# A split weight buffer of the experts, moved by 32 bytes

## The reference

```
probs = softmax(h @ router)
top_p, top_i = top_k(probs)                      # gates, made to sum to 1
for e in range(8):
    out += gates[:, e] * (silu(h @ w_gate[e]) * (h @ w_up[e])) @ w_down[e]
```

## Time and profile before

| | |
|---|---|
| timed runs | 1557.62, 1558.37, 1560.37 us (median 1558.37) |
| profiled execution, span | 1558.8 us (no time of it beside the span is recorded) |
| TensorE busy | 1525.1 us, 98% of the span |
| VectorE, ScalarE busy | 1188.6 us, 1017.6 us |
| expert stage | about 1130 to 1554 us |
| granted TensorE clock, mean | 0.995 of 2.4 GHz |

### The profile page before, as it was taken

How to read it: one execution, slowest core, us unless ns; L and a number is a source line. 1 busy time by engine, 2 the same in 40 slices (tenths; PEclk the granted TensorE clock), 3 DMA queues, 4 the chain that set the end, 5 groups by cost and what they waited for, 6 DMA issues and landing times.

```text
span 1558.8 us, 26842 instructions
## 1 busy us (share of the span) xinstructions
PE 1525.1 (98%) x9894; PEld 1308.5 (84%) x9894; DVE 1188.6 (76%) x1477; ACT 1017.6 (65%) x1431; POOL 60.4 (4%) x74
## 2 busy tenths in 40 slices
PE   7999999999999999999999999999999999999998
PEld 6988888878878888899888888998878888888886
DVE  5677877775578877787775556887688888888887
ACT  5667665566567656687465455875577777777775
POOL 0000000000000000020000000100000001101000
PEclk9999999999999999999999999999999999999999
DMA  7535455445424555464255555462699999999995
GB/s 269 195 119 189 167 211 188 177 147 189 169 102 165 213 188 184 142 190 144 80 192 187 204 181 184 162 167 83 227 373 368 394 387 381 369 396 385 364 362 210
DMA packets 54794, 351.08 MB, mean 225 GB/s; under 512 B 6208, under 2 KB 9968, under 8 KB 14896
## 3 DMA queue, kind: packets, MB, share of 16 engines
q1 hardware_dynamic: 46512, 330.94, 56.8%
q0 software_dynamic: 8192, 18.90, 4.7%
HBM read 341.90 MB, written 7.91 MB: 224 GB/s over the span
## 4 chain that ended last, share of the span: by engine, by line
PE 91%; DVE 4%; DMA 2%; ACT 2%; issue 1%; POOL 0%; SPq 0%; DVEq 0%; ACTq 0%
PE PS L917 20%; PE PS L1852 16%; PE PS L1985 14%; PE PS L2021 11%; PE PS L1870 8%; PE PS L1986 8%; PE PS L1478 1%; DVE EWL L3761 1%; PE PS L1083 1%; PE PS L1956 1%; DMA rows_m<-HN 1%; PE PS L1833 1%; DMA W<-in_weights 1%; PE PS L962 1%; PE PS L1547 1%
## 5 line engine op out<-in xcount | busy, mean ns | idle before, releaser
L3761 DVE TENSOR_TENSOR EWL<-W,EWH 128x2048 fp32r<-128x2048 f32 x144 | 329.6, 2291 | 45.4 <-ACT EWH L2789 45.2
L1985 PE MATMUL PS<-HTB,WH 128*128 128x512 f32 x944 | 329.3, 393 | 0.0
L2789 ACT ACTIVATE EWH<-W 128x2048 fp32r<-128x2048 f32 x144 | 276.5, 1920 | 61.3 <-PE PS L1870 34.2
L1986 PE MATMUL PS<-HTB,WL 128*128 128x256 f32 x1008 | 282.4, 280 | 0.0
L3087 DVE TENSOR_TENSOR WL<-W,WH 128x2048 fp32r<-128x2048 f32 x99 | 226.5, 2287 | 35.9 <-ACT WH L2216 32.8
L2216 ACT ACTIVATE WH<-W 128x2048 fp32r<-128x2048 f32 x99 | 189.2, 1918 | 95.4 <-PE PS L1986 84.6
L917 PE MATMUL PS<-MWH,HTB 128*128 128x256 f32 (+1 forms) x940 | 240.9, 341 | 2.1 <-issue 1.5
L3095 DVE TENSOR_TENSOR MWL<-W,MWH 128x1024 fp32r<-128x1024 f32 x136 | 164.5, 1220 | 85.2 <-ACT MWH L2240 83.2
L1985 PEld LDWEIGHTS PS<-HTB,WH 128*128 128x128 f32 x944 | 177.2, 188 | 40.1
L2240 ACT ACTIVATE MWH<-W 128x1024 fp32r<-128x1024 f32 x136 | 142.5, 1054 | 98.2 <-PE PS L917 89.8
L1986 PEld LDWEIGHTS PS<-HTB,WL 128*128 128x128 f32 x1008 | 189.5, 188 | 1.0
(11 more groups left out here) (413 smaller groups left out, 2441.1 us busy)
## 6 DMA issues: line engine op xcount, KB each, us to landing
W<-in_weights SPq DMA_DIRECT2D x311, 1024.0 KB, 4.9
CS<-in_consts POOLq DMA_DIRECT2D x4, 403.5 KB, 4.8
ARENA<-rows_m POOLq DMA_DIRECT2D x8, 192.0 KB, 6.2
ARENA<-rows_m POOLq DMA_DIRECT2D x2, 768.0 KB, 12.2
moe_acc<-X POOLq DMA_DIRECT2D x3, 512.0 KB, 12.1
moe_rows<-HN POOLq DMA_DIRECT2D x3, 512.0 KB, 12.1
X<-in_x SPq DMA_DIRECT2D x2, 512.0 KB, 4.4
W<-in_weights SPq DMA_DIRECT2D x2, 512.0 KB, 7.1
```

What stands on the lines that cost most here:

```text
L1985: mm(PS[b][:, :], WH[:, sl, o:o + P], HTB[:, :, kk, :], start=(kk == 0), stop=False, skip_group_check=True)
L1986: ins = mm(PS[b][:, 0:256], WL[:, sl, o:o + P], HTH[:, kk, :], start=False, stop=(kk == KC - 1), skip_group_check=True)
L2789: A(EWH[tile % SPLIT][:, :], tile_ap(w0 + tile), ACT.Copy).then_inc(sem("moe_hi"), 1)
L3761: TT(EWL[tile % SPLIT][:, :], tile_ap(w0 + tile), EWH[tile % SPLIT][:, :].bitcast(F32), SUB).then_inc(sem("moe_lo"), 1)
```

## The change

The experts' buffer 1 starts 8 floats (32 bytes) further on, both halves. To make room, every split buffer of every stage is given 16 floats more than it holds (`SHIFT_ROOM`), and a helper cuts the tensor out at a chosen offset. The tables `MIXER_SHIFT`, `FFN_SHIFT` and `MOE_SHIFT` hold the offsets in floats, and only the second entry of the last is not 0. The buffers become lists of tensors in place of one tensor with an index of its own; the instructions, their order and their waits stay as they are.

```diff
+SHIFT_ROOM = 16
+MIXER_SHIFT, FFN_SHIFT, MOE_SHIFT = (0, 0, 0), (0, 0, 0), (0, 8, 0)
...
+    nc.alloc_sbuf_tensor("HTB_END", [P, 2 * SHIFT_ROOM], F32)
...
+    nc.alloc_sbuf_tensor("W_END", [P, 2 * SPLIT * SHIFT_ROOM], F32)
...
-    ARENA_N = 21632
+    ARENA_N = 21632 + 6 * SHIFT_ROOM
...
+    def shifted(name, n, at, by):
+
+        return nc.alloc_sbuf_tensor_at(name, [P, n + SHIFT_ROOM], F32R, offset=at)[:, by:by + n]
+
+    half_step = 4 * (HALF + SHIFT_ROOM)
+    MWH = [shifted(f"MWH{k}", HALF, mw_at + k * half_step, MIXER_SHIFT[k]) for k in range(SPLIT)]
+    MWL = [shifted(f"MWL{k}", HALF, mw_at + (SPLIT + k) * half_step, MIXER_SHIFT[k]) for k in range(SPLIT)]
...
+    tile_step = 4 * (KC * TW + SHIFT_ROOM)
...
+    WH = [shifted(f"WH{k}", KC * TW, wh_at + k * tile_step, FFN_SHIFT[k]) for k in range(SPLIT)]
+    WL = [shifted(f"WL{k}", KC * TW, wl_at + k * tile_step, FFN_SHIFT[k]) for k in range(SPLIT)]
...
-    moe_lo_at = [dead_at + 4 * TILE_N, htl_at, arena_at + 4 * TILE_N]
-    EWH = [nc.alloc_sbuf_tensor_at(f"EWH{k}", [P, TILE_N], F32R, offset=o) for k, o in enumerate(moe_hi_at)]
-    EWL = [nc.alloc_sbuf_tensor_at(f"EWL{k}", [P, TILE_N], F32R, offset=o) for k, o in enumerate(moe_lo_at)]
-    moe_at = arena_at + 4 * 2 * TILE_N
+    moe_lo_at = [dead_at + 4 * step_n, ht_at + 4 * step_n, arena_at + 4 * step_n]
+    EWH = [shifted(f"EWH{k}", TILE_N, o, MOE_SHIFT[k]) for k, o in enumerate(moe_hi_at)]
+    EWL = [shifted(f"EWL{k}", TILE_N, o, MOE_SHIFT[k]) for k, o in enumerate(moe_lo_at)]
+    moe_at = arena_at + 4 * 2 * step_n
```

More of the change, by code:

```diff
@@ L171, in build @@
     HT = nc.alloc_sbuf_tensor_at("HT", [P, KC, S], F32, offset=ht_at)
-    MWH = nc.alloc_sbuf_tensor_at("MWH", [P, SPLIT, HALF], F32R, offset=mw_at)
-    MWL = nc.alloc_sbuf_tensor_at("MWL", [P, SPLIT, HALF], F32R, offset=mw_at + 4 * SPLIT * HALF)
-    assert 2 * SPLIT * HALF <= (RING - RAW) * KC * TW
+    def shifted(name, n, at, by):
[3 more added lines that the diff above has]
+    MWL = [shifted(f"MWL{k}", HALF, mw_at + (SPLIT + k) * half_step, MIXER_SHIFT[k]) for k in range(SPLIT)]
+    assert 2 * SPLIT * HALF <= (RING - RAW) * KC * TW and max(MIXER_SHIFT + FFN_SHIFT + MOE_SHIFT) <= SHIFT_ROOM
     ff_n = 6 * 2 * 512
-    gh_n, wh_n = 2 * 512, SPLIT * KC * TW
+    gh_n, wh_n = 2 * 512, SPLIT * (KC * TW + SHIFT_ROOM)
     assert ff_n + 2 * gh_n + 2 * wh_n <= ARENA_N
@@ L204, in build @@
     GAT = nc.alloc_sbuf_tensor_at("GAT", [P, NT, GAT_W], F32R, offset=moe_at + 4 * (2 * gr_n + 2 * xs_n + S))
-    moe_n = 2 * TILE_N + 2 * gr_n + 2 * xs_n + S + gat_n
+    moe_n = 2 * step_n + 2 * gr_n + 2 * xs_n + S + gat_n
     sel_at = -(-mx_at // 32) * 32
@@ L209, in build @@
     GAIN = nc.alloc_sbuf_tensor_at("GAIN", [P, D], F32, offset=sel_at)
-    YL = [nc.alloc_sbuf_tensor_at(f"YL{k}", [P, D // 2], F32R, offset=o) for k, o in enumerate((sel_at + 4 * D, dead_at + 8 * TILE_N))]
-    assert sel_at + 6 * D <= mx_at + 4 * N_MX and dead_at + 8 * TILE_N + 2 * D <= cs_at + 4 * CST["before"][0]
+    YL = [nc.alloc_sbuf_tensor_at(f"YL{k}", [P, D // 2], F32R, offset=o) for k, o in enumerate((sel_at + 4 * D, dead_at + 8 * step_n))]
+    assert sel_at + 6 * D <= mx_at + 4 * N_MX and dead_at + 8 * step_n + 2 * D <= cs_at + 4 * CST["before"][0]
     PS = [nc.alloc_psum_tensor(f"PS{b}", [P, 512], F32) for b in range(8)]
@@ L546, in build @@
     od.QN = v3(a(1024), 2)
+    a(SHIFT_ROOM)
     od.SM = a(2 * 1152).rearrange("p (u g k) -> p u g k", u=2, g=3)
@@ L995, in first_channel_half @@
                     o = k * TW + c * P
-                    ins = mm(bank(key)[:, c * 256:(c + 1) * 256], MWH[:, hf, o:o + P], HTL[:, 4 * hf + k, :], start=False,
+                    ins = mm(bank(key)[:, c * 256:(c + 1) * 256], MWH[hf][:, o:o + P], HTL[:, 4 * hf + k, :], start=False,
                              stop=(hf == 1 and k == KC // 2 - 1), skip_group_check=True)
@@ L1011, in first_pair_half @@
                         await_chunk(n, 2 * q + k)
-                    ins = mm(bank(keys[tt])[:, :], HTL[:, 2 * q + k, tt * P:(tt + 1) * P], MWH[:, q % SPLIT, k * 512:(k + 1) * 512],
+                    ins = mm(bank(keys[tt])[:, :], HTL[:, 2 * q + k, tt * P:(tt + 1) * P], MWH[q % SPLIT][:, k * 512:(k + 1) * 512],
                              start=False, stop=(q == 3 and k == 1), skip_group_check=True)
@@ L1955, in first_units @@
                         for n_w, wt in enumerate((WH, WL)):
-                            mm(PS[4 + c][:, 0:256], wt[:, sl, o:o + P], HTH[:, kk, :], start=(kk == 0 and n_w == 0),
+                            mm(PS[4 + c][:, 0:256], wt[sl][:, o:o + P], HTH[:, kk, :], start=(kk == 0 and n_w == 0),
                                stop=(kk == KC - 1 and n_w == 1), skip_group_check=True)
@@ L1962, in first_units @@
                         o = kk * TW + c * P
-                        ins = mm(PS[4 + c][:, 256:512], WH[:, sl, o:o + P], HTL[:, kk, :], start=False, stop=(kk == KC - 1),
+                        ins = mm(PS[4 + c][:, 256:512], WH[sl][:, o:o + P], HTL[:, kk, :], start=False, stop=(kk == KC - 1),
                                  skip_group_check=True)
@@ L1981, in up @@
                             if parted(gs, i):
-                                mm(PS[b][:, 0:256], WH[:, sl, o:o + P], HTH[:, kk, :], start=(kk == 0), stop=False, skip_group_check=True)
-                                mm(PS[b][:, 0:256], WH[:, sl, o:o + P], HTL[:, kk, :], start=False, stop=False, skip_group_check=True)
-                            else:
-                                mm(PS[b][:, :], WH[:, sl, o:o + P], HTB[:, :, kk, :], start=(kk == 0), stop=False, skip_group_check=True)
-                            ins = mm(PS[b][:, 0:256], WL[:, sl, o:o + P], HTH[:, kk, :], start=False, stop=(kk == KC - 1),
+                                mm(PS[b][:, 0:256], WH[sl][:, o:o + P], HTH[:, kk, :], start=(kk == 0), stop=False, skip_group_check=True)
+                                mm(PS[b][:, 0:256], WH[sl][:, o:o + P], HTL[:, kk, :], start=False, stop=False, skip_group_check=True)
+                            else:
+                                mm(PS[b][:, :], WH[sl][:, o:o + P], HTB[:, :, kk, :], start=(kk == 0), stop=False, skip_group_check=True)
+                            ins = mm(PS[b][:, 0:256], WL[sl][:, o:o + P], HTH[:, kk, :], start=False, stop=(kk == KC - 1),
                                      skip_group_check=True)
@@ L1996, in last_quarter @@
                             o = c * D + 512 + 256 * part
-                            ins = mm(out, gh[:, gs % 2, c, P:2 * P], wt[:, sl, o:o + 256], start=(part == 1 and c == 0 and n == 0),
+                            ins = mm(out, gh[:, gs % 2, c, P:2 * P], wt[sl][:, o:o + 256], start=(part == 1 and c == 0 and n == 0),
                                      stop=(c == 1 and n == 2), skip_group_check=True)
@@ L2215, in hi @@
                     await_full(act, ("od", "o", 3))
-            A(WH[:, j % SPLIT, :], tile_ap(t), ACT.Copy).then_inc(hi_done, 2)
+            A(WH[j % SPLIT], tile_ap(t), ACT.Copy).then_inc(hi_done, 2)
         def ffn_ahead(mixer):
@@ L2231, in hi_half @@
             if name == "ev" and h < 2:
-                A(rank_half(MWH[:, h, :]), rank_half(half_ap(name, h)), ACT.Copy).then_inc(hi_done, 1)
+                A(rank_half(MWH[h]), rank_half(half_ap(name, h)), ACT.Copy).then_inc(hi_done, 1)
                 return
@@ L2239, in hi_half @@
                     act.wait_ge(half_used, firsts_before[name] + u // 2 + 1)
-            A(MWH[:, h % SPLIT, :], half_ap(name, h), ACT.Copy).then_inc(hi_done, 1)
+            A(MWH[h % SPLIT], half_ap(name, h), ACT.Copy).then_inc(hi_done, 1)
         feeders = {n: Feeder(name, hi_half) for n, name in mixer_of_norm.items()}
@@ L3092, in lo_half @@
             if name == "ev" and h < 2:
-                TT(rank_half(MWL[:, h, :]), rank_half(half_ap(name, h)), rank_half(MWH[:, h, :].bitcast(F32)), SUB).then_inc(lo_done, 1)
+                TT(rank_half(MWL[h]), rank_half(half_ap(name, h)), rank_half(MWH[h].bitcast(F32)), SUB).then_inc(lo_done, 1)
                 return
-            TT(MWL[:, h % SPLIT, :], half_ap(name, h), MWH[:, h % SPLIT, :].bitcast(F32), SUB).then_inc(lo_done, 1)
+            TT(MWL[h % SPLIT], half_ap(name, h), MWH[h % SPLIT].bitcast(F32), SUB).then_inc(lo_done, 1)
         feeders = {n: Feeder(name, lo_half) for n, name in mixer_of_norm.items()}
```

18 lines of the change are left out of this document (9 added, 9 removed).

## The result

The changed kernel takes 1562.66 us (median of 10 runs, 1561.7 to 1563.74) against 1558.33 us before (10 runs): ratio 1.0026, 95% interval 1.0017 to 1.0036. It is 4.3 us slower, where 4.8 us less were forecast.

The account below looks back on a forecast made before the run. The prediction took TensorE's matmul stream to bound the kernel. Gains of 3.6, 1.15 and 0.05 us sum to 4.8 us, giving 1554.0 us by the profile or 1553.6 against the median, range 1552.3 to 1558.5.

Parts of the forecast that it names:

- What bounds the kernel: Whole kernel and expert stage: the stream of TensorE matmuls sets the time; TensorE is busy 1525.1 of 1558.8 us.
- The rest of the layout: Other buffers behind HTB move by 128 or 512 bytes and keep their position in 64 bytes: costed at nothing.
- Down tiles: Experts' 47 down calls of 12 matmuls on line 1870: 2.72 us each in place of 2.80, 3.6 us gained.
- the six behind them: First six matmuls behind each experts' down: 0.025 us gained each time, 1.15 us in sum.
- The third term: Second tile of the first expert group, also in buffer 1: 12 matmuls, 0.05 us gained.
- Feed and DMA: Expert stage: VectorE and ScalarE keep up, at most 0.105 us a group lost again; DMA costed at nothing.
- the bound on the copies: Copies writing the split buffers take the same time at either byte, so VectorE and ScalarE change by nothing.
- The second: Rival: a longer period, 128 bytes, makes 64-byte offsets mismatches elsewhere; slower, about 1562 us; 10%.
- The first rival: Buffer 1's distance from its partner or its region costs, not its place in 64 bytes; no change, 1558.4 us; 12%.

Follow-up runs that it names:

- first profile of before: Profile of the unchanged kernel, span 1558.8 us; the unchanged kernel was profiled a second time, span 1558.3 us, measured 1559.27 us.
- the kernel with room of 128: The changed kernel with 128 bytes of room behind each split buffer in place of 64: 1567.16 us, ratio 1.0054 to the kernel before.
- the mixers at 32 off: Old layout with the experts' buffer 1 moved 32 bytes, plus all six mixer buffers put 32 bytes off HTB: 1555.13 us, ratio 0.9982.
- buffer 1 alone: Kernel before with only the experts' buffer 1 moved up 32 bytes, other tensors keeping their place in 4096 bytes: 1554.33 us, ratio 0.9973.
- the kernel with buffer 1 16 off: Old layout with only the experts' buffer 1 moved, 16 bytes further up than the matched place, so 16 off its partners: 1557.16 us, ratio 0.9989.

## Why the prediction was wrong

**What bounds the kernel** was right. TensorE's stream of matmuls sets the time in every version, and what the intervals lost or gained came through to the end. No new wait appeared: in the experts' stage of the changed kernel TensorE waits 1.1 us for weights, against 0.6 in the earlier trace rows:

```profile
PE PS L1866 <- DVE EWL L3775: 1.1, 2, 0.9
```

**The step that failed** is in "The rest of the layout": "Position in 64 bytes stays for all of them, so I take nothing." The position that counts is that in 256 bytes. The rows of before could not tell 64 from 128 or 256, because every matched pair agreed in all three; the prediction said so of 128 and still costed the new spacing at nothing. It cost 5.0 us by itself, measured with buffer 1 left at its old place.

A slip in the addresses stands beside it. "All buffers behind `HTB` move by 128 bytes or 512" isn't so for `GRH`, `GRL`, `XH` and `XL`: they lie behind the two halves of buffer 2, each 64 bytes longer now, and move by 640. In 64 or 128 bytes nothing shows of that; in 256 it puts all six expert buffers off all four of them, the high halves by 128 and the low halves by 192, `EWH1` with them. With a move of 512 `EWH1` would have been matched.

**Down tiles** (3.6 us) and **the six behind them** (1.15 us) were sized right for a buffer that moves alone: the chain's pieces lose 3.5 us (126.07 - 122.61) and 1.0 us (65.53 - 64.54), the experts' stage 3.8 against the first profile of before and 4.3 against the second, and the medians of the runs differ by 4.0. In the change as made, with `EWH1` 128 off `GRH` and `EWL1` 192 off, `down` has 2.79: 125.55 us in sum, 0.5 less than before, while the pieces of 18, all of them off now, rose from 185.8 to 186.84. That is little for 18 matmuls: the first half of each piece stands behind transposes and was as slow or slower before. The third term, 0.05 us for one tile, is too small for the runs to tell.

**Feed and DMA**, costed at nothing, were right, and so was the bound on the copies: the copies that write the experts' low halves have a median of 2291 to 2293 ns at every byte tried.

**The rivals.** The second is what happened in kind, a longer period, and it had been given 10%. Its period was not right: 128 bytes is refuted by the kernel with room of 128, which is slower still. That its size fits too (1561.7 to 1564 forecast, 1562.66 measured) is in good part luck. Dense `down`, the mixers' 512 columns as a loss and their 256 as a gain of 3 ns do show in the lines after. But the 2.6 us that it gave back for a cured `down` came to 0.5, and the 2.7 it took for `EWL` in `up` came to 1.0 over all pieces of 18. The line of those matmuls, 388/392/400 before, hardly moved:

```profile
L1866 PE MATMUL PS<-EWL,XH x384: 387/393/402, 1131.7 to 1545.7; 128*128 128x512 f32 x192
```

What it didn't have is dense `up`, 350 ns a pair after (232 + 117.5) against 347 before. Nor was its gain of 3 ns for 256 columns read from like rows: 283 stood in a stream of 256 columns and 280 in the mixed one, where a match measured 281; the mixers at 32 off did then show the 3 ns. The first rival, distance or region, is refuted by buffer 1 alone: 32 bytes cured it where it lies. The rule of the Trainium skill that was weighed ("TensorE: Matmul & The Clock Gate", Part 2: weight loads have a read port of their own and take nothing from the running matmul) would make all kernels here equal. They differ by up to 16.3 us (1567.16 - 1550.85), with only places changed. That the weight load and the moving operand get in each other's way inside the memory fits this, but it was only argued; no run parts it from another mechanism that looks at the two addresses.

**Why the chance was too low**: the one case that priced the rest of the layout got 10%, though the prediction said of it that nothing excludes it. No row supported 64 over 128 or 256; an unknown that all rows leave open should have been given something near even odds.

## What to carry to other kernels

A change of addresses touches every tensor behind the first one that moves: list them all with their difference to the operand they are multiplied with, before and after, in the longest period that the rows can't exclude. To move one buffer without moving the rest, pad by a large power of two (4096 bytes here). Then tune the offset for each stream of matmuls by itself: of the offsets tried, streams of 512 columns were best at 0, of 256 at 64 and mixed ones at 32 bytes, and no single one served all three.

## What the runs showed of the hardware

The interval between fp32r matmuls, each with a weight load of its own, depends on the offset (weights less partner, modulo 256 bytes; differences of 256 in 512 were free). For 512 columns after each other: 227 ns at 0, 231 at 16, 233 at 128, 234 at 224 (the experts, kernel before) and at 32 (the mixers); at 64 the mixers have 231 with the high half and 226 to 229 with the low. For 256 columns after each other, with `HTB` moving: 120 at 0, 117 at 32, and at 64 stretches at 113 and others at 118, in two mixers of one kernel with the same addresses. For 512 and 256 in turn: 353 ns a pair at 0, 347 at 32, 353 at 64 (235 + 118). The numbers of one width are medians or their averages, those of pairs means. Where matched and unmatched pairs take turns, the matched ones are slow too (230 and 236 ns, with the low halves 128 off).

Behind two transposes, matched matmuls need nine places to come back to 227 ns (224 to 236 until then), and two places in the kernel with buffer 1 16 off, where the matmuls before the transposes ran in another rhythm. So an interval also depends on what the stream did before.

Why a match is best for one width and worst for another stays open, as does what sets the rate at 64; the offsets 96, 160 and 192 were seen only mixed with others.
